# Leaving out the constant products that TensorE makes ahead of the eight norms of a two-block network

## The reference

```python
def rmsnorm(x, g):
    xf = x.astype(jnp.float32)
    y = xf * lax.rsqrt(jnp.mean(xf * xf, axis=-1, keepdims=True) + EPS) * g.astype(jnp.float32)
    return y.astype(x.dtype)

# first_block: eight norms in all, by the kernel's names
h = rmsnorm(x, g_mix)                       # "nx"
kv_m = rmsnorm(mem, g_mem) @ w_mem_kv       # "nm"
x = x + merged @ w_out
h2 = rmsnorm(x, g_ffn)                      # "nf"
x = x + peer_ffn(h2, ...)
return rmsnorm(x, g_final)                  # "nl"
# hybrid_layer, for l = 0 and 1
h = rms_norm(x, norm1_g)                    # "n1.0", "n1.1"
x = x + (mix @ w_out)
h = rms_norm(x, norm2_g)                    # "n2.0", "n2.1"
gt, up = jnp.split(h @ w_ffn_in, 2, axis=-1)
x = x + ((jax.nn.silu(gt) * up) @ w_ffn_out)
```

## Time and profile before

| | before |
|---|---|
| runs, median (lowest to highest) | 2426.42 us (2425.41 to 2430.86), 3 runs |
| the profiled execution's own time | 2424.03 us |
| its span from first to last instruction | 2422.7 us |
| mean granted TensorE clock | 0.973 of full speed |
| TensorE busy | 2232.2 us, 92% of the span, 15186 records |
| VectorE, ScalarE, GpSimd busy | 67%, 49%, 36% |
| records at line 581 (the sets) | 128, 32.1 us in the sum by form |

### The profile page before, as it was taken

How to read it: one execution, slowest core, us unless ns; L and a number is a source line. 1 busy time by engine, 2 the same in 40 slices (tenths; PEclk the granted TensorE clock), 3 DMA queues, 4 the chain that set the end, 5 groups by cost and what they waited for, 6 DMA issues and landing times.

```text
span 2422.7 us, 38114 instructions
## 1 busy us (share of the span) xinstructions
PE 2232.2 (92%) x15186; PEld 2068.3 (85%) x15186; DVE 1631.0 (67%) x2519; ACT 1193.9 (49%) x2040; POOL 877.8 (36%) x477
## 2 busy tenths in 40 slices
PE   8888889999999789999997798999999699898999
PEld 8887879999999678888886697889988588787997
DVE  6768742778544986666658789586655968777664
ACT  5546444454444975554552454535444255545443
POOL 5554457777200950000034474440004546442000
PEclk9999999999999999999998898899999899999999
DMA  6443445655556026666653344345664435334665
GB/s 222 131 122 112 133 152 178 183 162 179 179 185 184 12 76 194 192 194 195 194 175 126 121 144 131 105 141 163 184 190 145 131 106 156 112 116 150 183 186 160
DMA packets 102931, 369.59 MB, mean 153 GB/s; under 512 B 11362, under 2 KB 13794, under 8 KB 102116
## 3 DMA queue, kind: packets, MB, share of 16 engines
q1 hardware_dynamic: 102756, 367.15, 49.3%
HBM read 364.49 MB, written 2.62 MB: 152 GB/s over the span
## 4 chain that ended last, share of the span: by engine, by line
PE 62%; DVE 28%; ACT 5%; issue 3%; DMA 2%; POOL 1%; SPq 0%; DVEq 0%; ACTq 0%
PE stream_bank L530 10%; PE stream_bank L531 10%; PE stream_bank L532 10%; PE side_bank L530 9%; PE side_bank L531 9%; PE side_bank L532 9%; DVE conv_out L2030 6%; DVE first_hot L1970 2%; DVE unit_lo L1568 2%; DVE experts L1960 2%; ACT unit_hi L1048 1%; PE side_bank L592 1%; DVE S L1638 1%; DVE gates L1673 1%; POOL unit_lo L2302 1%
## 5 line engine op out<-in xcount | busy, mean ns | idle before, releaser
L2302 POOL TENSOR_TENSOR unit_lo<-raw,unit_hi 128x1024 fp32r<-128x1024 f32 (+1 forms) x305 | 754.0, 2481 | 519.1 <-ACT unit_hi L1048 518.8
L1048 ACT ACTIVATE unit_hi<-raw 128x1024 fp32r<-128x1024 f32 (+1 forms) x678 | 707.2, 1045 | 189.9 <-PE side_bank L532 82.6
L1568 DVE TENSOR_TENSOR unit_lo<-raw,unit_hi 128x1024 fp32r<-128x1024 f32 x373 | 459.3, 1232 | 390.6 <-ACT unit_hi L1048 390.0
L530 PE MATMUL stream_bank<-hT_hi,unit_hi 128*128 128x256 f32 x1672 | 501.4, 300 | 7.4 <-DVE unit_lo L1568 6.9
L531 PE MATMUL stream_bank<-hT_lo,unit_hi 128*128 128x256 f32 x1672 | 483.3, 289 | 0.0
L532 PE MATMUL stream_bank<-hT_hi,unit_lo 128*128 128x256 f32 x1672 | 482.5, 289 | 0.0
L530 PEld LDWEIGHTS stream_bank<-hT_hi,unit_hi 128*128 128x128 f32 x1672 | 332.2, 199 | 17.2 <-DVE unit_lo L1568 7.3
L531 PEld LDWEIGHTS stream_bank<-hT_lo,unit_hi 128*128 128x128 f32 x1672 | 331.9, 198 | 2.1
L532 PEld LDWEIGHTS stream_bank<-hT_hi,unit_lo 128*128 128x128 f32 x1672 | 330.9, 198 | 0.0
L530 PE MATMUL stream_bank<-h2T_hi,unit_hi 128*128 128x256 f32 x1152 | 327.4, 284 | 2.6 <-DVE unit_lo L1568 2.5
L531 PE MATMUL stream_bank<-h2T_lo,unit_hi 128*128 128x256 f32 x1152 | 326.7, 284 | 0.0
(11 more groups left out here) (354 smaller groups left out, 4260.6 us busy)
## 6 DMA issues: line engine op xcount, KB each, us to landing
raw<-in_peer_u_dram SPq DMA_DIRECT2D x128, 512.0 KB, 3.6
raw<-in_peer_v_dram SPq DMA_DIRECT2D x128, 512.0 KB, 3.6
raw<-in_gate_dram SPq DMA_DIRECT2D x64, 512.0 KB, 3.6
raw<-in_gt_dram SPq DMA_DIRECT2D x44, 512.0 KB, 3.6
raw<-in_up_dram SPq DMA_DIRECT2D x44, 512.0 KB, 3.7
raw<-in_ffn_out_dram SPq DMA_DIRECT2D x44, 512.0 KB, 4.2
raw<-in_branch_dram SPq DMA_DIRECT2D x32, 512.0 KB, 3.6
raw<-in_w_gate_dram SPq DMA_DIRECT2D x24, 512.0 KB, 3.6
```

The lines of the kernel that those rows point to most:

```text
L530: mm(out, l.hi, r.hi, start=start, stop=False)
L1048: activation(k.unit_hi[n % SPLIT_SLOTS][:, 0:w], k.raw[n % RAW_SLOTS][:, 0:w], ACT.Copy).then_inc(k.sem("unit_hi"), 1)
L1568: V.tensor_tensor(k.unit_lo[s][:, 0:w], k.raw[n % RAW_SLOTS][:, 0:w], k.unit_hi[s][:, 0:w], ALU.subtract).then_inc(unit_lo, 1)
L2302: G.tensor_tensor(k.unit_lo[s][:, 0:w], k.raw[n % RAW_SLOTS][:, 0:w], k.unit_hi[s][:, 0:w], ALU.subtract).then_inc(k.sem("unit_lo_pool"), 1)
```

## The change

`keep_warm`, its constant and its operand are taken out, and with them the eight calls. Nothing is put in their place, nothing else moves: the order of the remaining instructions on every engine, all transfers, all buffers and the waits of `norm_turns` stay as they are.

```diff
-KEEP_WARM = 8
@@ tiles
-        self.warm = base[:, 0:2 * P]
@@ pe_program
-    def keep_warm(name):
-        bank = take(SIDE + 4, ("warm", name))
-        for _ in range(KEEP_WARM):
-            last = mm(bank[:, 0:TOKENS], k.ident, k.warm, start=True, stop=True)
-        last.then_inc(k.free[SIDE + 4], 1)
-
@@ mixer
         pe.wait_ge(k.sem("landed_base"), 32)
-        keep_warm("nm")
         pe.wait_ge(k.sem("landed_m_in"), 16)
@@ token_norm
-            keep_warm("nx")
             yield
@@ peer
-        keep_warm("nf")
         for _ in norm_turns(k.X, "nf"):
             pass
...
             tm_unit("peer_v", j, one, 0, 1, 1024, banks, j == 0, j == KEYS - 1)
-        keep_warm("nl")
@@ layer
-        keep_warm(name("n1"))
         for _ in norm_turns(k.X, name("n1")):
             pass
...
-        keep_warm(name("n2"))
         for _ in norm_turns(k.X, name("n2")):
             pass
```

## The result

The changed kernel takes 2440.07 us (median of five runs, 2438.11 to 2441.96) against 2426.42 us before (now five runs, 2425.34 to 2430.86). The ratio is 1.0056, with a 95% interval of 1.0042 to 1.0069: slower by 13.6 us, 10.2 to 16.7 us by the interval. The forecast was 2436.2 us in a range of 2430 to 2443. The sign, the mechanism at the late norms and the range held; the sum was 3.9 us short, and three of its terms were wrong in ways that cancel in part.

A forecast was written before the change was run, and what follows sets the result against it. TensorE, busy 92% of the span, was taken as the bound where its work came last. Late restarts +9.4, "nf" +0.4 and the start 0 gave +9.8 us on 2426.4: 2436.2 us, range 2430 to 2443.

The forecast's parts named there:

- A set saves nothing in line at the six late places: At "nf", "nl", "n1.0", "n2.0", "n1.1", "n2.1" turns wait for VectorE's diagonal, not the set; removal in line gains 0.
- The clock comes down in gaps of 4.3 us and more, and a restart costs 2.34 us: At "n1.0", "n2.0", "n1.1", "n2.1" four restarts fall to the half level: +9.4 us; bounds 1.7 and 3.9 us each.
- Nothing behind covers it: Behind the late turns, waits move along and TensorE has no slack, so each restart's 2.34 us is lost in full.
- "nf" pays already, +0.4 us: At "nf" the restart already runs partly at the half level; longer idle time adds +0.4 us, bounds 0 and 0.4.
- "nm" and "nx" come to 0, with the wait at 74.56 us as cover: At the start, TensorE's wait on VectorE ending at 74.56 us absorbs shifts: 0 us, bounds -0.7 and +0.6.
- The range: Whole kernel: 2430 (one restart escapes, others cheap) to 2443 us (restarts of 3.9 us each).
- More costly restarts: Rival at the four late norms: restarts cost 3.9 us each, +16.1 us in all, 2442.5 us; chance 0.12.
- Turns that don't bring the clock up: Rival at the late norms: turns don't count towards the full clock, +26 us, 2452 us; chance 0.02.
- Only the long gap: Rival: only "n1.0" with its 8.5 us gap falls, +2.7 us, 2429.1 us; chance 0.09.
- Faster by the set in line: Rival at "nx": its set delays TensorE's work, so removal gains 3.3 us, 2423.1 us with no restart falling; chance 0.04.

The follow-up runs named there:

- experiment 2: Only the sets of "nm" and "nx" left out, against the kernel before: ratio 1.0022 (1.0012 to 1.0032), +5.3 us.
- experiment 5: Only the set of "nx" left out, against the kernel before: ratio 1.0009 (0.9996 to 1.0022), +2.2 us.

## Why the prediction held, and where its steps failed

- *A set saves nothing in line at the six late places.* Right. The turns still start behind the diagonal, and idle time grew by 2.8 to 3.9 us for a set of 3.62 us, and by 7.3 us for the two ahead of "n1.0".
- *The clock comes down in gaps of 4.3 us and more, and a restart costs 2.34 us.* Right. 2.2, 2.1, 1.7 and 2.4 us in the changed kernel. The price taken from the eight other gaps was the step that carried the forecast. (Its other half, that a set keeps the clock up, was read at the late norms; at "nm" the set did so in five of nine profiles, and in four the turns took 5.4 to 6.8 us.)
- *Nothing behind covers it.* Right behind "n2.0" and "n2.1" (+2.1 us each, groups that don't touch). Not tested in the prediction for the mixing stages, where the row it quoted doesn't reach: behind "n1.0" +1.4 us, and behind "n1.1" +4.7 us, twice the term. Among the late norms this is the term that was most mis-sized, by 2.4 us: later in that stretch the clock is down for longer as well, by 3.3 us in the mean. Behind "n1.0" it is the other way round, and part of the restart is given back.
- *"nf" pays already, +0.4 us.* Of the right size, but not shown: the table has +0.2 us, within the scatter. The turns took 6.47 us instead of 5.44, yet in six other profiles with the full set of eight they took 5.85 to 6.26 us, so the profile of the kernel before was the mildest of its kind.
- *"nm" and "nx" come to 0, with the wait at 74.56 us as cover.* This step failed: +5.3 us in experiment 2, +3.3 us in the table. The cover is a wait on VectorE, and the prediction held VectorE's path for fixed. It said itself that VectorE comes to this wait from small operations behind the same diagonal; what it missed is that one of them lengthens eightfold when GpSimd is ahead of it. The 0.7 us of delay between diagonal and turns, whose end it counted as a gain, is what had kept GpSimd behind. The gain itself didn't come: the diagonal was written 0.7 us later, as it had allowed for a clock that comes up late, and the turns started at 26.14 us in place of 26.08. Its bound of +0.6 us for the two sets was too low by 2 us or more; how the rest of the loss divides is open.
- *The range.* It held by luck in part. The forecast's own range ended at about +13 us, and the measured +13.6 us lies beyond it; the end at 2443 us was put there for restarts of 3.9 us each, which did not occur.
- *Rivals.* More costly restarts: not as priced (2.8 us, at "nf", was the dearest in the changed kernel's profile), though by another way the total came to their side. Turns that don't bring the clock up: refuted, all came back within 8 us in the changed kernel's profile. Only the long gap: refuted by every profile that leaves out the other sets. Faster by the set in line: refuted by experiments 2 and 5.

## What to carry to other kernels

Work whose result nobody reads can be worth its place: look at the granted clock behind an idle gap before calling it waste, and price a restart from the other gaps of the same trace. A wait on another engine is cover only if that engine's path stays as it is; where VectorE and GpSimd run side by side, a shift of a few tenths of a microsecond can change it. Where single executions of the same instructions differ by 7 us over one stage, cut the profiles of many kernels at the same instructions and compare stretch by stretch, with the time at the half level beside each.

## What the runs showed of the hardware

- A set of constant products keeps the clock up by the time that it keeps TensorE at work, not by being issued. Eight products of 256 columns (3.62 us) left turns of 3.81 us at the four norms from "n1.0" on, in every profile; the same count with 16 columns (1.85 us) left 5.4 to 6.6 us, and four products of 256 columns (1.89 us) left 5.44 us at three of the four.
- Gaps between 2.3 and 3.5 us go either way. In one execution 2.44 us was let pass, 2.78 us and 3.24 us were not; in another 2.93 us and 3.53 us were let pass and 2.30 us was not.
- Executions of the same instructions differ by time at the half level: up to "nf" 8.0 us were lost to it in a profile of 351.5 us and 15.4 us in one of 358.7 us.
- A VectorE operation of 0.29 us took 2.34 us when it started 0.28 us behind a GpSimd operation of 2.47 us, and ended 0.15 us after it.
